# Gate chain spread over three weight groups, memory's products moved to VectorE, value banks of the second attention swapped

## What is computed

```
h = x
h = h + W_out @ groupnorm(mLSTM | HGRN2 | Fourier | neighbourhood attention)(rms_norm(h) @ W_in)
h = h + CrossAttn(rms_norm(h), mem_n),   mem_n = rms_norm(mem, norm_mem)
h = h + HierarchicalMoE(rms_norm(h))     # 32 experts, top 2
out = rms_norm(h)

# mLSTM, four gates of 4 heads each, from a slice mg of the first product
bcum = cumsum(log_sigmoid(fg));  m_t = max(inter, max(dmat));  w = exp(dmat - m_t)
h    = num / max(|den|, exp(-m_t))
```

## Time and profile before

| | us |
|---|---|
| median of 3 runs | 1872.28 |
| lowest, highest | 1871.53, 1872.79 |
| the profiled execution's own time | 1873.4 |
| its span | 1871.6 |
| TensorE busy | 1724.3 (92%) |
| VectorE busy | 840.5 (45%) |
| ScalarE busy | 522.3 (28%) |
| GpSimd busy | 64.8 (3%) |

### The profile page before, as it was taken

How to read it: one execution, slowest core, us unless ns; L and a number is a source line. 1 busy time by engine, 2 the same in 40 slices (tenths; PEclk the granted TensorE clock), 3 DMA queues, 4 the chain that set the end, 5 groups by cost and what they waited for, 6 DMA issues and landing times.

```text
span 1871.6 us, 26055 instructions
## 1 busy us (share of the span) xinstructions
PE 1724.3 (92%) x10706; PEld 1088.5 (58%) x10706; DVE 840.5 (45%) x1165; ACT 522.3 (28%) x747; POOL 64.8 (3%) x33
## 2 busy tenths in 40 slices
PE   7989999999999999999799988899888898988996
PEld 7879899899777899978543332233323233232332
DVE  5566555798666454354643232232322323232233
ACT  5453443644354453344411000011000110000102
POOL 0004000033000000000000000000000000000001
PEclk9999999999999999999899999999999999999998
DMA  8753645444455565338499999999999999999995
GB/s 325 253 178 106 223 159 179 148 153 143 150 176 180 182 193 177 116 135 315 166 402 423 427 427 428 428 429 428 428 428 429 428 429 428 429 428 429 428 428 229
DMA packets 105393, 561.03 MB, mean 300 GB/s; under 512 B 9696, under 2 KB 9824, under 8 KB 79200
## 3 DMA queue, kind: packets, MB, share of 16 engines
q1 hardware_dynamic: 95808, 436.13, 59.7%
q10 hardware_dynamic: 9504, 123.74, 15.7%
HBM read 557.75 MB, written 2.10 MB: 299 GB/s over the span
## 4 chain that ended last, share of the span: by engine, by line
PE 67%; DMA 27%; DVE 3%; ACT 1%; issue 1%; SPq 0%; ACTq 0%; DVEq 0%
DMA arena<-in_moe_w_dram 27%; PE ps L970 14%; PE ps L617 7%; PE ps L619 6%; PE ps L618 6%; PE ps L611 6%; PE ps L612 6%; PE ps L613 6%; PE ps L1000 5%; PE ps L982 2%; PE ps L1017 2%; PE ps L916 1%; DVE w_lo L1575 1%; PE ps L858 1%; PE ps L839 1%
## 5 line engine op out<-in xcount | busy, mean ns | idle before, releaser
L970 PE MATMUL ps<-arena 128*64 128x512 f32 x2048 | 504.6, 627 | 84.1 <-DMA arena<-in_moe_w_dram 82.5
L1575 DVE TENSOR_TENSOR w_lo<-arena,w_hi 128x1024 fp32r<-128x1024 f32 x264 | 331.4, 1297 | 237.8 <-ACT w_hi L1145 237.6
L1145 ACT ACTIVATE w_hi<-arena 128x1024 fp32r<-128x1024 f32 x264 | 265.1, 1054 | 309.3 <-PE ps L613 169.4
L970 PEld LDWEIGHTS ps<-arena 128*64 128x64 f32 x2048 | 138.1, 142 | 346.4 <-issue 252.9
L2200 DVE TENSOR_TENSOR arena<-ps,arena 128x1024 f32<-128x1024 f32 x128 | 156.7, 1225 | 274.0 <-PE ps L1017 274.0
L1000 PE MATMUL ps<-arena 128*64 128x512 f32 x1024 | 225.6, 593 | 5.2 <-DVE arena L2177 3.2
L611 PE MATMUL ps<-x_hi,w_hi 128*128 128x256 f32 x512 | 148.4, 290 | 19.0 <-DVE w_lo L1575 19.0
L1000 PEld LDWEIGHTS ps<-arena 128*64 128x64 f32 x1024 | 73.2, 137 | 149.3 <-issue 139.5
L612 PE MATMUL ps<-x_lo,w_hi 128*128 128x256 f32 x512 | 147.5, 288 | 0.0
L613 PE MATMUL ps<-x_hi,w_lo 128*128 128x256 f32 x512 | 147.4, 288 | 0.0
L1430 ACT ACTIVATE arena<-ps 128x512 f32<-128x512 f32 x64 | 38.3, 599 | 385.3 <-PE ps L970 385.3
(11 more groups left out here) (363 smaller groups left out, 2409.7 us busy)
## 6 DMA issues: line engine op xcount, KB each, us to landing
arena<-in_moe_w_dram SPq DMA_DIRECT2D x133, 2048.0 KB, 20.1
arena<-in_moe_w_dram ACTq DMA_DIRECT2D x58, 2048.0 KB, 14.1
arena<-in_w_in_dram SPq DMA_DIRECT2D x52, 1024.0 KB, 5.1
arena<-in_xa_wk_dram SPq DMA_DIRECT2D x16, 1024.0 KB, 5.0
arena<-in_xa_wv_dram SPq DMA_DIRECT2D x16, 1024.0 KB, 5.0
arena<-in_w_out_dram SPq DMA_DIRECT2D x16, 1024.0 KB, 5.0
arena<-in_xa_wq_dram SPq DMA_DIRECT2D x16, 1024.0 KB, 5.0
arena<-in_xa_wo_dram SPq DMA_DIRECT2D x16, 1024.0 KB, 5.2
```

The source lines that it names most:

```text
L970: last = mm(ps[rows_, m, :], xe[par][:, ECH * i + c, :], ring_up[m][i][:, c, :], start=(i == 0 and c < 2), stop=(i == ECH - 1 and c >= 2))
L1145: fn(hi_ring[(2 * n + u) % 4][:], ring_a[i][:, 2 * u:2 * u + 2, :], ACT.Copy).then_inc(S["w_hi"], 1)
L1575: V.tensor_tensor(w_lo[i][:, 2 * u:2 * u + 2, :], ring_a[i][:, 2 * u:2 * u + 2, :], hi_ring[(2 * n + u) % 4][:].bitcast(F32), ALU.subtract ...
```

## The change

It has four parts. The gate chain's eight steps on VectorE move from turn g = 4 to turn g = 5, ScalarE's last Exp moves from turn g = 4 to turn g = 6 ahead of `high(6, (2, 3))`, the 16 small products move from behind group 5 to behind group 6 and into bank 5, and VectorE's copy of them from turn g = 6 to turn g = 7. The eight products on memory leave GpSimd for VectorE: two in turn 4, one in turn 6, two in turn 7, one each in turns 8, 9 and 10. The banks of the second attention's values are swapped, and TensorE's wait for all four heads becomes a wait for three ahead of group 29 and for the fourth ahead of its chunk 3. A wait of ScalarE for `na_y` ahead of `high(G_WO, (0,))` is dropped.

```diff
+MEM_ROWS, MEM_GAINS = {6: (2,), 7: (3,)}, {7: (0,), 8: (1,), 9: (2,), 10: (3,)}
...
-            pool.wait_ge(S["mem_t_in"], 16)
-            pool.wait_ge(S["front_in"], 16)
-            pool.wait_ge(S["rms_row"], 2)
-            for n in range(NCH):
-                at = mem_t[:, CH * n:CH * (n + 1), :]
-                nc.gpsimd.tensor_tensor(at, at, bc_mid(mem_rms, CH), ALU.mult).then_inc(S["m_rows"], 1)
-            for n in range(NCH):
-                at = mem_t[:, CH * n:CH * (n + 1), :]
-                pool.wait_ge(S["m_rows"], n + 1)
-                nc.gpsimd.tensor_tensor(at, at, bc_last(cols[:, 3 * KT + CH * n:3 * KT + CH * (n + 1)], T), ALU.mult).then_inc(S["m_gain"], 1)
...
-                        last = mm(bank(4, NT, 4, NH)[:, j, kind, :], gr[:, kind, j * P:(j + 1) * P], ident[0:NH, 0:NH],
+                        last = mm(bank(5, NT, 4, NH)[:, j, kind, :], gr[:, kind, j * P:(j + 1) * P], ident[0:NH, 0:NH],
...
-                pe.wait_ge(S["gate_dve"], 4)
...
-                if g == G_ML - 2:
+                if g == G_ML - 1:
                     ml_gates()
-                if g == G_ML - 1:
                     ml_ready()
...
-                        last = mm(bank(2 * (hd % 2) + c // 2, 2, T)[:, c % 2, :], v[:, s, (4 * hd + c) * P:(4 * hd + c + 1) * P],
+                        last = mm(bank(2 - 2 * (hd % 2) + c // 2, 2, T)[:, c % 2, :], v[:, s, (4 * hd + c) * P:(4 * hd + c + 1) * P],
...
-            pe.wait_ge(S["xs_oa"], XA_H)
-            pe.wait_ge(S["xs_od"], XA_H)
+            def mixed(heads):
+                pe.wait_ge(S["xs_oa"], heads)
+                pe.wait_ge(S["xs_od"], heads)
...
+            mixed(XA_H - 1)
             for n in range(4):
...
-                dense_split(G_XO + n, False, split[G_XO], part=[2, 3])
+                dense_split(G_XO + n, False, split[G_XO], part=[2])
+                if n == 0:
+                    mixed(XA_H)
+                dense_split(G_XO + n, False, split[G_XO], part=[3])
...
-                    act.wait_ge(S["gate_dve"], 3)
-                    fn(gr[:, 2:4, :], gr[:, 2:4, :], ACT.Exp, scale=-1.0).then_inc(S["gate_act"], 1)
...
+                if g == G_ML - 1:
+                    act.wait_ge(S["gate_dve"], 3)
+                    fn(gr[:, 2:4, :], gr[:, 2:4, :], ACT.Exp, scale=-1.0).then_inc(S["gate_act"], 1)
...
-            act.wait_ge(S["na_y"], 16)
             high(G_WO, (0,))
...
-                if g == 3:
+                if g == 4:
 
                     dve.wait_ge(S["gate_dve"], 2)
                     dve.wait_ge(S["gate_act"], 1)
...
+            def memory_rows(part):
+                for n in part:
+                    at = mem_t[:, CH * n:CH * (n + 1), :]
+                    V.tensor_tensor(at, at, bc_mid(mem_rms, CH), ALU.mult).then_inc(S["m_rows"], 1)
+            def memory_gains(part):
+                for n in part:
+                    at = mem_t[:, CH * n:CH * (n + 1), :]
+                    dve.wait_ge(S["m_rows"], n + 1)
+                    V.tensor_tensor(at, at, bc_last(cols[:, 3 * KT + CH * n:3 * KT + CH * (n + 1)], T), ALU.mult).then_inc(S["m_gain"], 1)
...
-                if g == G_ML - 1:
+                if g == G_ML:
                     dve.wait_ge(S["gate_pe"], 3)
-                    V.tensor_copy(mlc.rearrange("p j k h -> p (j k h)"), ps[:, 4, 0:NT * 4 * NH]).then_inc(S["gate_dve"], 1)
-                if g == G_ML:
+                    V.tensor_copy(mlc.rearrange("p j k h -> p (j k h)"), ps[:, 5, 0:NT * 4 * NH]).then_inc(S["gate_dve"], 1)
...
+                    dve.wait_ge(S["mem_t_in"], 16)
+                    memory_rows((0, 1))
+                if g in MEM_ROWS:
+                    memory_rows(MEM_ROWS[g])
+                if g in MEM_GAINS:
+                    memory_gains(MEM_GAINS[g])
```

More of the change, by code:

```diff
@@ L1363, in xa_out_hi @@
             def xa_out_hi(hd):
-                b0 = 2 * (hd % 2)
+                b0 = 2 - 2 * (hd % 2)
                 act.wait_ge(S["xs_o"], hd + 1)
```

## The result

| | before | after |
|---|---|---|
| median of 4 runs, us | 1872.53 | 1861.07 |
| lowest and highest, us | 1871.53, 1873.71 | 1860.61, 1861.58 |
| profiled execution, us | 1873.4 | 1861.58 |
| its span, us | 1871.6 | 1859.7 |

The ratio is 0.9933, with a 95% interval from 0.9922 to 0.9945: 12.5 us less by it, 11.5 by the medians. 1861.0 was predicted.

The account below looks back on a forecast made before the run. TensorE was taken to set the pace until slice 20, the experts' transfers following it. Gains of 6.8 + 1.7 + 0.4 + 2.4 = 11.3 us took the profiled 1873.4 to 1862.1, hence a median of 1861.0; range 1857.5 to 1865.0.

Parts of the forecast that it names:

- What bounds it: TensorE sets the pace before slice 20; the experts' transfers then wait for it, so early gains pass on in full.
- the sum: Whole kernel: 6.8 + 1.7 + 0.4 + 2.4 = 11.3 us less, giving 1861.0; within 1.3 us, chance 0.60.
- The wait ahead of group 5: TensorE's 7.65 us wait there shrinks to about 0.8 us once the gate chain moves: gain 6.8 us.
- The low clock behind it: Behind TensorE's start on group 5, the clock of 0.50 goes along with the long wait: gain 1.7 us.
- What is late next: VectorE's 5.1 us chain in turn 5 stays hidden with 1.7 us to spare; ScalarE's Exp in turn 6 is hidden.
- Group 7: TensorE's 0.36 us wait there for a load that SyncE held until the masks were converted goes: gain 0.4 us.
- The dip of the small products: The 0.50 clock behind the gates' 16 products moves with them: cost 0, bounds 1.6 us gained or lost.
- Rival A: The clock falls elsewhere as matmuls from group 5 on come earlier; each dip about 1.6 us, 1857.8 to 1864.2; chance 0.20.
- Memory's products: Eight products on VectorE at 1.22 us each, 9.8 us in all, lie beside idle time: cost 0.
- Rival D: Slower: VectorE's products delay low parts; over 5.4 us each they eat the gain, at 6 us 1874.9; chance 0.02.
- The banks: Swapped banks of the second attention's values remove TensorE's pause ahead of group 29: gain 2.4 us, bounds 0 to 2.4.
- rival B: Only the gate part pays, as a low part becomes due at group 29: 1863.4 us; chance 0.06.

Follow-up runs that it names:

- eight more products: The changed kernel with eight more 128x1024 products on VectorE in turn 4, ahead of group 5's first low part, into unused memory: 1868.38 us, ratio 0.9974.
- memory alone: The kernel before with only memory's eight products moved from GpSimd to VectorE: 1872.26 us, ratio 0.9999.
- the chain alone: The kernel before with only the gate chain spread and its small products in bank 5; memory's products stay on GpSimd, banks stay: 1865.03 us, ratio 0.9954.
- The second profile: The changed kernel itself run once more, nothing altered: 1862.7 us, ratio 0.9935.
- the chain with memory: The kernel before with the gate chain spread and memory's products on VectorE, without the edits of the second attention: 1862.57 us, ratio 0.9945.
- dealt out: The changed kernel with the 16 small products placed four behind each of group 6's four chunks: 1860.98 us, ratio 0.9935.
- late Ln with dealt products: The changed kernel with ScalarE's Ln behind group 5's first high part and the 16 small products spread over group 6's chunks: 1860.06, then 1860.28 us.

## Why the prediction was right, point by point

**What bounds it.** Right. The front's gain reached the end: 12.72 us at the first expert, 12.15 at the last matmul. From the first expert's matmul to the start of TensorE's last matmul it is 939.1 us before and 939.6 after, and from 936.9 to 939.5 in the profiles of the eleven experiments, which reach the first expert between 906.4 and 918.0. So the second half passes gains on, with a scatter of its own of some 3 us, about as large as the smaller terms of the sum.

**The wait ahead of group 5**, 6.8 by the sum. Measured: 8.12 earlier, of which 1.14 were there at the end of group 4 already and are no effect of the change (below): 6.98, or 7.65 - 0.67. The working held in each step: from ScalarE's start to the low part 129.83 - 128.75 = 1.08 us (1.14 expected), to TensorE 131.20 - 128.75 = 2.45 (2.5). The assumption that the low part is quick without GpSimd holds, 1.16 us.

**The low clock behind it**, 1.7 by the sum: 9.84 - 8.12 = 1.72. It went with the wait, and returned with it in the kernel with eight more products. Its size isn't fixed: of 6.8 us of low clock each time, 3.9 us lay beside matmuls in the kernel before, 3.0 with memory alone and 5.1 with eight more products, and the rest in the pause. Behind 0.67 us of idling it stayed at 1.00, in all four profiles that have that pause. The argument for it, that the 2.42 us ahead of group 29 had no low clock behind them either, was weaker than it read: with the chain alone the same pause had one (last section).

**What is late next.** The chain ends at 151.55 in turn 5, and the low part at 151.48 + 1.17 = 152.65. Its chunk is due two chunks behind 143.04, at 143.04 + 2 x 5.76 = 154.6: 1.9 us to spare, where 1.7 were given. The moved Exp costs nothing: ScalarE idles 1.81 us behind it.

**Group 7.** The 0.36 us of waiting are gone, as the sum has it; the load that SyncE holds for the masks has landed in time: ScalarE's idling ahead of group 7's first high part (9.44 us) is now ended by TensorE and no longer by the load.

**The dip of the small products**, "travels with them": 0, bounds 1.6 either way. In the first profile it did, 3.4 us before and after, so the term was 0. But that was one draw. The second profile had 6.8, the chain with memory none, so both bounds occur, and this term is what scatters the time of the kernels behind this change. The prediction's reading of it, that the row cannot tell the place from the chance, was right; the experiments tell: it comes with the 16 in one piece (none when dealt out, three times), and its length differs between executions of one program. Rival A thus was no rival but a part of the spread. The Trainium skill ("TensorE: Matmul & The Clock Gate", Part 1) says of a kernel's first matmuls that the number of cold ones differs from run to run of the same kernel. The start shows this here (the last paragraph of this section), and 3.4 and 6.8 us behind the same instructions are a variation of the same kind, at a place of which that sentence doesn't speak.

**Memory's products.** Cost 0: right, 0.9999. They take 1.18 us each in turn 4 (2.36 / 2), 1.22 elsewhere. Rival D would have needed 5.4.

**The banks**, 2.4 by the sum. In the profile 12.54 - 9.89 = 2.65: the pause of 2.42, and some 0.2 with which the matmuls behind it ran closer. Alone they made 1.9 by the medians. No low part or load became due in their place, so rival B falls; that the chain with memory ended level with the changed kernel is within the spread of both.

**The sum.** 6.98 + 1.72 + 0.36 + 2.65 = 11.7 us, where 11.3 were predicted. The first three make 9.06, and that is what the first product of the Fourier part shows: 10.20 - 1.14 = 9.06. From there to the second attention 0.3 us are lost, and nothing that was run tells to what. The third high part of group 29 is 12.54 earlier, and without the 1.14 at the start 11.4. The 1.14 come from the first 18 us of the program: in the profile of before the matmuls of the first group take 0.41 us each until about 16.9 us, and 0.28 from then on; in that of after the change comes at about 14.2. (The granted clock reads 1.00 in both there, so this rests on the durations.) Nothing of the change stands there, and group 4 of the changed kernel's second profile ends 0.8 us later again (132.03 - 0.67 = 131.36). That the median came within 0.1 us of 1861.0 is better than the method: two terms, the start and the experts' stretch, scatter by 1 to 3 us between executions, and cancelled here.

## What to carry to other kernels

Where an engine with an ordered list holds a short chain that waits for another engine, look at what is queued behind each of its steps: here one Exp of 0.63 us, waiting for a chain of 5.1, cost 7 us of TensorE's time and another 1.7 of low clock behind the wait, and moving it one or two groups on, into idle time, made both good. Cost a move by the margin of what becomes due next, as a subtraction of two rows, and check it by taking the cover away; a margin of 1.7 us was 1.9. And don't book a single dip of the clock as a gain or a loss of one edit: in two profiles of one program it differed by a factor of two.

## What the runs showed that was not expected

The clock fell while TensorE was never idle, behind 16 matmuls of 4x4 that take 1.94 us, and for 0, 3.4 or 6.8 us. The same 16 behind another group, in one run, did nothing.

It also falls behind pauses that the prediction had down as harmless. TensorE's timeline with the chain alone, at group 29, with the clock behind it; then in the changed kernel, at a group behind the neighbourhood attention; then the same place one head earlier, in the second series of the late Ln with dealt products, again with the clock:

```profile
795.65 0.77 PE L617 MATMUL ps<-w_hi,o_hi 128*128 128x512 f32 x1 [2.42 <-issue]
...
796.00:797.00 1.00, 1.00 (x3) 0.50 0.06 16
```

```profile
573.60 0.47 PE L608 MATMUL ps<-w_hi,y_hi 128*128 128x512 f32 x1 [2.73 <-DVE w_lo L1572]
...
574.00:577.40 3.40, 3.40 (x10) 0.51 0.87 359
```

```profile
560.23 0.51 PE L608 MATMUL ps<-w_hi,m_hi 128*128 128x512 f32 x1 [0.89 <-DVE w_lo L1582]
...
561.00:562.00 1.00, 1.00 (x4) 0.50 0.37 139
```

The pause of 2.42 us ahead of group 29 stands in four profiles (before, chain alone, memory alone, chain with memory), and in one of them 3.4 us of low clock follow. The 2.73 us have such a dip behind them in all thirteen profiles. The 0.89 us, which have short matmuls ahead of them (128x64 and 64x256), had one once, and 0.98 us in such surroundings once, at 488 us. So a pause that is hidden in no transfer costs itself and, by a chance that differs from place to place, some 1.6 us more, and behind the long waits ahead of group 5 up to 2.4. What sets that chance wasn't tried.

A low part on VectorE and one of GpSimd's products (L518) slow each other down. Alone they take some 1.2 and 2.41 us, side by side 3.42 and 3.41 (the chain alone), which is about as long as one behind the other, 1.2 + 2.4 = 3.6. Whether TensorE notices depends on which low part is hit: the one that it waited for took 1.40 us, and the slow ones behind it were hardly late. Slow did not mean on the path.
